# Latent attention moved beside the dense products of the last three projections, outputs as rows; the attention keeps two groups

## What is computed

```python
h = rms_norm(x, norm1[l])
proj = h @ w_in[l]
(a_cq, a_ckv, a_kr, b_q, b_k, b_v, c_q, c_k, c_v, c_qi, c_ki, c_w, d_q, d_k, d_v, d_f) = split_cols(proj)
qa = (rms_norm(a_cq, mla_q_norm[l]) @ mla_w_uq[l]).reshape(B, S, H, MLA_NOPE + MLA_ROPE)     # 64 + 32
q_a = jnp.concatenate([qa[..., :MLA_NOPE], rope(qa[..., MLA_NOPE:], pos)], axis=-1)
kv = (rms_norm(a_ckv, mla_kv_norm[l]) @ mla_w_ukv[l]).reshape(B, S, H, MLA_NOPE + MLA_V)
k_a = jnp.concatenate([kv[..., :MLA_NOPE], jnp.broadcast_to(k_rope, (B, S, H, MLA_ROPE))], axis=-1)
o_a = causal_block_attention(q_a, k_a, kv[..., MLA_NOPE:], (MLA_NOPE + MLA_ROPE) ** -0.5)   # A: latent
o_b = sliding_window_attention(q_b, k_b, v_b, swa_sinks[l], Dh ** -0.5)                      # B: window 128
o_c = dsa_attention(q_c, k_c, v_c, qi, ki, c_w, top_k, Dh ** -0.5)                           # C: 128 chosen keys
o_d = causal_block_attention(d_q, d_k, d_v, Dh ** -0.5, log_f_cum=cum)                       # D: forget gates
x = x + concat(o_a, o_b, o_c, o_d) @ w_out[l]
x = x + jnp.square(jax.nn.relu(rms_norm(x, norm2[l]) @ w_up[l])) @ w_down[l]
```

## Time and profile before

| | us |
|---|---|
| median of 3 runs | 1926.37 (1924.74 to 1927.21) |
| profiled execution | 1931.15, its span 1929.3, mean granted TensorE clock 0.979 |
| fourth, fifth, sixth job, first layer | start at 99.13, 126.56, 155.56; end at 187.93 |
| attention, first layer | 187.93 to 291.05 (103.1) |
| of it D, A, C | pair starts at about 188, 205.65; 225.57, 240.89; 254.55 |
| last scores to first product of the output job | 277.62 to 291.05 |
| attention, second layer | 873.17 to 973.64 (100.5) |

### The profile page before, as it was taken

The page is one execution under the profiler, slowest core; times in us unless marked ns, Lnnn a source line. Parts: engine busy times, 40 slices in busy tenths (PEclk is TensorE's granted clock), DMA queues, the critical chain, the costliest instruction groups (busy, mean ns, idle before and its releaser), DMA issues.

```text
span 1929.3 us, 22937 instructions
## 1 busy us (share of the span) xinstructions
PE 1852.3 (96%) x9006; PEld 1476.0 (77%) x9010; DVE 912.9 (47%) x1555; ACT 651.9 (34%) x1172; POOL 740.5 (38%) x326
## 2 busy tenths in 40 slices
PE   7999889999999999998899999999999999999997
PEld 6678557788888886786577888888788888888786
DVE  3667762424141426688624534436521124339374
ACT  4534351322121245343423222212434443443212
POOL 5232243444444443332333544444333233235342
PEclk9999899999999999997999999999999999999999
DMA  7224002232232233120024343343332222322211
GB/s 220 66 66 164 1 1 86 75 103 87 91 105 87 70 94 108 49 83 1 1 66 164 100 157 123 134 154 99 94 127 88 66 66 90 109 66 88 88 66 44
DMA packets 104441, 170.89 MB, mean 89 GB/s; under 512 B 21615, under 2 KB 39431, under 8 KB 103208
## 3 DMA queue, kind: packets, MB, share of 16 engines
q1 hardware_dynamic: 103320, 169.79, 27.0%
q10 hardware_dynamic: 1040, 0.00, 0.0%
HBM read 166.56 MB, written 7.93 MB: 90 GB/s over the span
## 4 chain that ended last, share of the span: by engine, by line
PE 88%; DVE 6%; ACT 2%; issue 2%; POOL 0%; DMA 0%; SPq 0%; DVEq 0%; ACTq 0%
PE G L2010 25%; PE G L2012 25%; PE G L2011 25%; PE S L2272 2%; PE S L1053 1%; DVE neg_max L1882 1%; DVE select L1846 1%; PE G L2308 1%; PE S L2055 1%; ACT prob L1497 1%; PE S L1027 1%; DVE work L1682 1%; PE S L1038 1%; PE G L2289 1%; DVE top L1681 1%
## 5 line engine op out<-in xcount | busy, mean ns | idle before, releaser
L1283 POOL TENSOR_TENSOR w_lo<-raw,w_hi 128x1024 fp32r<-128x1024 f32 x272 | 678.0, 2513 | 1011.2 <-ACT w_hi L1320 688.1
L1320 ACT ACTIVATE w_hi<-raw 128x2048 fp32r<-128x2048 f32 x96 | 183.8, 1915 | 543.7 <-PE G L2012 543.7
L2010 PE MATMUL G<-h_hi,w_hi 128*128 128x512 f32 x896 | 359.9, 402 | 2.1 <-DVE h_lo L810 2.1
L2012 PE MATMUL G<-h_hi,w_lo 128*128 128x512 f32 x896 | 354.8, 396 | 0.0
L2011 PE MATMUL G<-h_lo,w_hi 128*128 128x512 f32 x896 | 354.7, 396 | 0.0
L2010 PE MATMUL G<-w_hi,h_hi 128*128 128x512 f32 (+2 forms) x704 | 281.4, 400 | 6.6 <-issue 4.9
L2012 PE MATMUL G<-w_hi,h_lo 128*128 128x512 f32 (+2 forms) x704 | 272.1, 386 | 0.0
L2011 PE MATMUL G<-w_lo,h_hi 128*128 128x512 f32 (+2 forms) x704 | 271.6, 386 | 0.0
L2012 PE MATMUL G<-w_hi,u_lo 128*128 128x512 f32 x512 | 204.2, 399 | 0.0
L2010 PEld LDWEIGHTS G<-h_hi,w_hi 128*128 128x128 f32 x896 | 168.5, 188 | 45.0 <-DVE h_lo L810 2.9
L2011 PE MATMUL G<-w_lo,u_hi 128*128 128x512 f32 x512 | 201.7, 394 | 0.0
(11 more groups left out here) (314 smaller groups left out, 2247.7 us busy)
## 6 DMA issues: line engine op xcount, KB each, us to landing
raw<-in_w_in_dram SPq DMA_DIRECT2D x40, 1024.0 KB, 5.4
raw<-in_w_up_dram SPq DMA_DIRECT2D x32, 1024.0 KB, 5.3
raw<-in_w_down_dram SPq DMA_DIRECT2D x32, 1024.0 KB, 5.0
raw<-in_w_out_dram SPq DMA_DIRECT2D x12, 1024.0 KB, 5.0
w_ada<-in_w_ada_dram SPq DMA_DIRECT2D x4, 3072.0 KB, 11.9
skew_scratch<-line_scratch SPq DMA_DIRECT2D x1, 4608.0 KB
raw<-in_w_in_dram SPq DMA_DIRECT2D x8, 512.0 KB, 4.5
raw<-in_w_in_dram SPq DMA_DIRECT2D x4, 832.0 KB, 6.7
```

The lines of the kernel that those rows point to most:

```text
L1283: ins = pool.tensor_tensor(w_lo[:, c % SPLIT_SLOTS, part], raw[:, c % RAW_SLOTS, part], w_hi[:, c % SPLIT_SLOTS, part].bitcast(F32), ALU.s ...
L1320: act.activation(w_hi[:, c % SPLIT_SLOTS], raw[:, c % RAW_SLOTS], ACT.Copy).then_inc(high_ready, 1)
L2010: pe.matmul(dst, a_hi, b_hi, start=first, stop=False)
L2012: return pe.matmul(dst, a_lo, b_hi, start=False, stop=last)
```

## The change

Group A's eight items leave the attention and are hosted in the fourth to the sixth job beside B's. `SIDE` gets Q (a pair's queries or keys turned to columns, into `qkT_a`), A (an item, two steps like P) and N (its output rows `rows_oa` turned to columns). The output of A is now computed as rows, as B's is. `PAIRS` is D and C, 16 items; the last pair's query tiles run from the widest to the narrowest. M moves from the head of the attention into the jobs, and F goes last. `rows_b` is rotated in two halves, at the chores of A01 and A03 (group, pair, query tile), `rows_c` at those of P01, P02, P03, P10. 40 rounds of the index selection run ahead of the attention instead of 32. The high part of a weight piece (`MID_PIECE`) that stood at the end of the attention is made in two parts at items 2 and 4 and its low part in four behind POOL's scalings 5, 6, 7 and 9.

```diff
-PAIRS = [(g, hp) for g in "DAC" for hp in range(2)]
-ITEMS = [(p, qt) for p in range(len(PAIRS)) for qt in range(TT)]
+PAIRS = [(g, hp) for g in "DC" for hp in range(2)]
+ITEMS = [(p, TT - 1 - n if p == len(PAIRS) - 1 else n) for p in range(len(PAIRS)) for n in range(TT)]
...
-EARLY_SPLITS = {20: (0,), 21: (1,), 22: (2,), 23: (3,)}
+MID_HIGH = {2: slice(0, 2), 4: slice(2, 4)}
+MID_LOW = {5: 0, 6: 1, 7: 2, 9: 3}
+MID_PIECE = 2 * (JOB_V + 1) + 1
+EARLY_SPLITS = {NI - 4: (0,), NI - 3: (1,), NI - 2: (2,), NI - 1: (3,)}
...
-SIDE = ([("L",)] + [("U", t) for t in range(TT)] + [("K",)]
-        + [("P", hp, qt) for hp in range(2) for qt in range(TT)] + [("F",), ("M",)])
+SIDE = ([("L",)] + [("U", t) for t in range(TT)]
+        + [item for hp in range(2) for item in
+           [("Q", hp, "q"), ("Q", hp, "k")] + [("A", hp, qt) for qt in range(TT)]]
+        + [("K",)] + [("P", hp, qt) for hp in range(2) for qt in range(TT)] + [("N",), ("M",), ("F",)])
 NS = len(SIDE)
 AT = {item: n for n, item in enumerate(SIDE)}
-NB = 2 * TT
+NB = 4 * TT
...
-          JOB_B: {1: 1, 6: 1, 11: 1, **spread(12, 32, side_steps(0, AT["K",]))},
-          JOB_C: spread(14, 32, side_steps(AT["K",], AT["K",] + 3)),
-          JOB_D: spread(0, 32, side_steps(AT["K",] + 3, AT["K",] + 6)),
-          JOB_V: spread(0, 32, side_steps(AT["K",] + 6, AT["M",]))}
+          JOB_B: {1: 1, 6: 1, 11: 1, **spread(12, 32, side_steps(0, AT["Q", 0, "q"]))},
+          JOB_C: spread(1, 32, side_steps(AT["Q", 0, "q"], AT["A", 1, 0])),
+          JOB_D: spread(0, 32, side_steps(AT["A", 1, 0], AT["P", 0, 2])),
+          JOB_V: spread(0, 32, side_steps(AT["P", 0, 2], NS + 1))}
 LAYER_SC = NB + NI
 LAYER_OV = NI
-EARLY_ROUNDS = 2 * ROUNDS
+EARLY_ROUNDS = 5 * ROUNDS // 2
...
+            def part_low(number, c, k):
+                pool.wait_ge(high_ready, number + 1)
+                ins = pool.tensor_tensor(w_lo[:, c % SPLIT_SLOTS, k], raw[:, c % RAW_SLOTS, k],
+                                         w_hi[:, c % SPLIT_SLOTS, k].bitcast(F32), ALU.subtract)
+                if k == HALF_K - 1:
+                    ins.then_inc(low_ready, 1)
...
+                    if i in MID_LOW:
+                        part_low(number + MID_PIECE, MID_PIECE, MID_LOW[i])
+                for c in range(MID_PIECE + 1, FIRST_GROUP_PIECE):
...
+                    elif kind == "Q":
+                        scale = LATENT_SCALE if SIDE[n][2] == "q" else 1.0
+                        ins = act.activation(latent_columns(n, 1), bank(n, 1)[0:MLA_QK], ACT.Copy, scale=scale)
                     else:
-                        ins = act.activation(mixT_bc[:, 1, :], bank(n, 1), ACT.Copy)
+                        dst = mixed("B" if kind == "M" else "A", 1)
...
+                def part_high(part):
+                    c = MID_PIECE
+                    act.wait_ge(raw_loaded[c % RAW_SLOTS], l * LAYER_LOADS[c % RAW_SLOTS] + loads_upto(c))
+                    act.wait_ge(bank_filled, (jobs + PROJ_JOBS) * TT)
+                    ins = act.activation(w_hi[:, c % SPLIT_SLOTS, part], raw[:, c % RAW_SLOTS, part], ACT.Copy)
+                    if part.stop == HALF_K:
+                        ins.then_inc(high_ready, 1)
...
-                    if i == NI - 1:
-                        ahead(JOB_V, 1)
+                    if i in MID_HIGH:
+                        part_high(MID_HIGH[i])
...
-                    if n == AT["K",] - 1:
-                        stored(JOB_B)
-                        rotate(rows_b[:, :, 0:384].rearrange("p t (h d) -> p t h d", h=6), rope64, 6, 32)
-                        dve.engine_nop().then_inc(window_ready, 1)
-                    if n == AT["K",] + 3 and not output:
+                        if t == TT - 1:
+                            dve.engine_nop().then_inc(latent_ready, 1)
+                    if n in (AT["A", 0, 1], AT["A", 0, 3]) and not output:
+                        first = 2 if n == AT["A", 0, 3] else 0
+                        if not first:
+                            stored(JOB_B)
+                        rotate(rows_b[:, :, 0:384].rearrange("p t (h d) -> p t h d", h=6), rope64, 6, 32, first, first + 2)
+                        if first:
+                            dve.engine_nop().then_inc(window_ready, 1)
+                    if n == AT["P", 0, 1] and not output:
                         stored(JOB_C)
-                    if output and AT["K",] + 3 <= n <= AT["K",] + 2 + TT:
-                        rotate_c(n - AT["K",] - 3)
+                    if output and n - AT["P", 0, 1] in range(TT):
+                        rotate_c(n - AT["P", 0, 1])
...
+                        dst = rows_oa[:, qt, P * hp:P * hp + P].rearrange("p (h d) -> p h d", h=2)
...
+                def side_scores(n):
+                    kind, hp, qt = SIDE[n]
+                    tiles = side_tiles(n)
+                    q, k = slice(P * qt, P * qt + P), slice(P * tiles[0], P * (qt + 1))
+                    if kind == "P" and n == AT["K",] + 1:
                         pe.wait_ge(even_taken, evens + (EVEN[n - 1, "t"] + 1))
+                    elif kind == "A" and qt == 0:
+                        pe.wait_ge(even_taken, evens + (EVEN[n - 1, "s"] + 1))
+                    if qt == 0 and not scored(n - 1):
                         pe.wait_ge(odd_taken, odds + (ODD[n - 1, "s"] + 1))
                     for e in range(2):
-                        at = slice(HD * e, HD * e + HD)
-                        pe.matmul(bank(n, e)[:, 0:P * len(tiles)], qkT_b[at, 2 * hp, P * qt:P * qt + P],
-                                  qkT_b[at, 1, P * tiles[0]:P * (qt + 1)], start=True, stop=False)
-                    mask = window_few[:, 0 if qt else P:2 * P]
+                        if kind == "A":
+                            queries, keys = (qkT_a[hp][e + at][0:MLA_QK] for at in (0, 2))
+                        else:
+                            queries, keys = (qkT_b[HD * e:HD * e + HD, at, :] for at in (2 * hp, 1))
+                        pe.matmul(bank(n, e)[:, 0:P * len(tiles)], queries[:, q], keys[:, k], start=True, stop=False)
...
+                    kind, hp, _ = SIDE[n]
+                    tiles = side_tiles(n)
                     for e in range(2):
+                        rows, at = (mla_v, HD * (2 * hp + e)) if kind == "A" else (rows_b, 384 + HD * e)
                         for b, kb in enumerate(tiles):
                             ins = pe.matmul(bank(n, 0)[:, HD * e:HD * e + HD], prob_b[n % 2][e][:, P * b:P * b + P],
-                                            rows_b[:, kb, 384 + HD * e:384 + HD * e + HD], start=b == 0, stop=b == len(tiles) - 1)
+                                            rows[:, kb, at:at + HD], start=b == 0, stop=b == len(tiles) - 1)
...
-                assert AT["M",] % 2 and AT["M",] == NS - 1
                 give_qk(0, range(qk_units(0)))
-                advance(1)
-                pe.wait_ge(odd_taken, odds + (ODD[AT["M",], "s"]))
+                pe.wait_ge(odd_taken, odds + ODDS)
                 give_scores(0)
-                pe.wait_ge(even_taken, evens + EVENS)
-                pe.wait_ge(odd_taken, odds + ODDS)
```

165 lines of the change are left out of this document (92 added, 73 removed).

## The result

The changed kernel took 1932.57 us (median of 9 runs, 1928.89 to 1934.09) against 1926.50 (9 runs): a ratio of 1.0027, 95% interval 1.0018 to 1.0036, so about 5 us slower by the ratio, 6 by the medians. The profiled execution took 1930.56 us, span 1928.7, mean clock 0.979, which is no slower than the profiled execution before (1931.15).

What follows compares the result with a forecast made beforehand. PE's stream was taken as the bound (88% of the chain), plus its few waits. Terms of -4.5 us in the first layer and -2.4 in the second gave -6.9, from the median 1926.37 to 1919.5; range 1909 to 1932.

Steps and rivals of the forecast that it cites:

- D's second pair: Attention: fewer transposes to host and no index rounds after the fourth item; -5.2 us first layer, -1.6 second.
- GpSimd's low parts: Attention: four low parts of the weight piece between GpSimd's scalings, one delaying the next item; +0.3 us a layer.
- Group A: -29.0: Attention: the section of group A's eight items disappears, -29.0 us a layer.
- +27.3 of PE work: Fourth to sixth job: group A's items, Q, N and M return between dense products, +27.3 us a layer.
- The waits on DVE: Hosting jobs: PE waits for DVE slowed by rotations, +4.2 us in the sixth, +1.8 in the fourth, a layer.
- The 1.0 for meetings of a rotation with a weight split: Sixth job: rotations slowed from 0.42 to 2.60 us beside GpSimd's weight split; 1.0 us allowed of 2.2.
- F at the end, +0.6, less 0.4: Head of the attention: F last leaves DVE and ACT less time, M gone saves 0.4; net +0.2 us.
- From one execution to the median: Whole kernel: 1924.2 us from the profiled execution, less 4.8 for the median of runs, gives 1919.5.
- The tail, -4.1: Last scores to output job: 13.4 becomes 7.6 us, against scores coming 1.7 later; net -4.1 us.
- The signs: Disproof: job waits above 9.5 us a layer, clock below 0.95 in fourth or fifth job, tail over 11 us.
- DVE as the bound at 13.5 us of waits: Rival, the jobs: items outpace DVE, PE waits 13.5 us a layer instead of 6; 1934.5 us, chance 0.14.
- The second rival: No net gain: half the gain of tail and D's second pair stays a DVE wait; 1927 us, chance 0.25.

Runs made afterwards that it cites:

- e1: The kernel before, unchanged, run and profiled a second time: median 1927.52 us, this profiled execution 1926.84 us.
- e13: The changed kernel, unchanged, run and profiled a second time: median 1930.74 us, ratio 1.0017 to before.
- e8: The changed kernel with 45 of the 48 index rounds a layer left out, so group C attends to wrong keys: 1899.49 us.
- e12: e2 with all 48 index rounds ahead of the attention instead of 32: 1925.11 us.
- e7: The changed kernel with its hosted steps dealt 13, 13, 14 to the last three jobs instead of 12, 12, 16: 1923.67 us, ratio 0.9989 to before.
- e6: The kernel before with only the weight piece's high and low parts made inside the attention: 1918.39 us, ratio 0.9952.
- e3: The changed kernel with the reversed last pair and the weight piece's split inside the attention both undone: 1942.10 us, ratio 1.0071 to before.
- e2: The kernel before with only the reversed last pair and the weight piece split inside the attention: 1915.19 us, ratio 0.9938.

## Why the prediction was wrong

It said 1919.5, range 1909 to 1932, faster at 0.52; measured 1932.57. The step that failed most is D's second pair, -5.2 and -1.6 us: it started from a stretch that was slow by the clock (19.92 us, 17.54 in e1), left out that DVE has more to do in D's first two items than in A's (2.7 us) and took the end of the half clock as given (4.6 us in one layer of two). The second is the head of the attention with F uncovered, +0.2, which measured +1.7 to +3.1. The ledger against e1, the execution of before that lies near the median:

| us | forecast | first layer | second layer |
|---|---|---|---|
| fourth job to the first scores | +33.5, +32.0 | +36.8 (128.70 - 91.87) | +38.2 (130.10) |
| GpSimd's low parts | +0.3 | in the rows below | in the rows below |
| D, first pair | 0 | 0.0 | +0.1 |
| D, second pair | -5.2, -1.6 | +3.4 (20.94 - 17.54) | -1.2 |
| group A | -29.0 | -29.0 | -29.0 |
| C, first pair | 0 | -1.7 (12.78 - 14.49) | -1.7 |
| C, second pair and tail | -4.1 | -5.5 (16.69 - 22.17) | -5.7 |
| sum | -4.5, -2.4 | +4.1 | +0.9 |

+4.9 in all. The two executions compared differ by 3.6 us in their spans (1928.7, 1925.1), so -1.3 lie outside these stretches, in pieces of up to 2 us of either sign; the ratio of all runs, 1.0027, is +5.2.

- **"Group A: -29.0" and "+27.3 of PE work"** held. Summed over PE's timeline, the hosted blocks without their waits grew by 27.6 us in the first layer (18.0 to 45.6), and by 26.8 in the first layer of e13, where no block lies at the half clock. Queries, scores and outputs came near their forecast prices: 0.79 for eight transposes, 4.3 against 4.5 for a pair's scores, 4.1 for a pair's outputs.
- **The waits on DVE, "6.0"**, measured 5.1 and 4.1 more than before, and 6.5 in the first layer of e13, where the clock is full: PE's slow stretches and its waits take each other's place, since DVE sets the sixth job's length (43.4 of 45.35 us busy). In the fourth A01's rotation cost 0.8 and A03's nothing, where I had 1.0 and 0.8. The 1.0 for meetings of a rotation with a weight split was wrong in place: none of the 36 instructions of the rotations took over 0.56 us. The split met the two-column addition instead, and PE's wait behind it is 1.7.
- **Missing from the sum: the interval behind a block.** I priced a block up to the next dense start, but the interval behind that is 0.32 and not 0.23; the earlier trace rows end at that start. 39 blocks instead of 17: +2.0 us a layer.
- **"F at the end, +0.6, less 0.4"**: wrong in size. From the start of the last dense product to the first scores, before takes 4.17 us, the changed kernel 5.9 in the first layer and 7.3 in the second, where the clock is 0.76 under F. That is +1.7 and +3.1 where I had +0.2. In the first layer PE waits there 0.57 us for DVE's `fox_k` and 0.89 for its `qkT`, where e1 has 0.32 for `qkT` alone. The dip of the clock in the sixth job, which looks like a second missing term, costs nothing: the job is as long without it.
- **"D's second pair, -5.2"**: the step that failed most. First, 19.92 was no fair measure of before: e1 has 17.54. Second, A's second pair was no fair measure of what would be left. Its last two items take the same 5.59 us as those of D's second pair in the quick form, but its first two 8.07 where D's take 10.75 at either clock: DVE is busy for 7.78 us there with three index rounds in it, and for 10.00 with four in D's. With no rounds D's two items take 7.67 (e8) and 8.17 (e12, first layer). What I added to A's 13.7, 1.0 and 2.2 us, I had put down to the clock; it is 2.7, and it is DVE's. Third, I took the end of the half clock as given, and the last two items lie at the full clock or the half, 5.59 or 10.19 us. So the pair is 13.7 + 2.7 = 16.3, or 4.6 more. Quick form against quick form, the lighter pair is worth 1.2 us (17.54 to 16.34), near my -1.6 for the second layer; slow against slow it is 1.0 longer. What picks the one or the other was not settled: e7's profile has neither layer slow, which is too few to say that dealing the steps differently avoids it.
- **From one execution to the median.** I subtracted the 4.8 us by which the profiled execution exceeded the median, and counted as gains two stretches in which that execution was slow (2.4 of D's pair, 1.5 of the second layer's sixth job). These 3.9 us were in effect counted twice.
- **"The tail, -4.1"** was right in mechanism and somewhat too small. Against e1 the stretch from the last scores to the output job fell from 13.59 to 7.20 us, -6.4 where I had -5.8, and these scores came 0.9 later, not 1.7: -5.5. e6 shows that the weight piece is the larger part. The 1.7 us of C's first pair, forecast at nothing, e3 gives without the tail edits.
- **The signs.** Those that would make the prediction wrong did not come: PE's waits were 6.1 and 5.2 us a layer, the clock 1.00 in the fourth and fifth job, the last scores to the output job 7.2. The expected sizes held for the jobs (123.05 against 122) and not for the attention, 70.7 and 67.3 us from the last dense product on against 65 and 66. The list had no sign for the head or for D's pairs, where it failed.
- **The rivals.** DVE as the bound at 13.5 us of waits is not what happened, though in the sixth job alone DVE is the bound. The second rival, in which half of the gain in tail and D's second pair stays a wait on DVE, is right for D's pair, whose first two items DVE sets; the tail gave all. A rival in which the half clock gets worse in the attention, not in the jobs, was missing.

The version that beats both is e2: before with the two tail edits, 12 us under before and 17 under the changed kernel. Against e7, the quickest form of the move that keeps the whole computation, it is 8 us ahead.

## What to carry to other kernels

Work of PE that is moved between dense products keeps its price: what can be won is only the idle time of the section it leaves (here 3.4 of 29 us), and 22 more interruptions at 0.09 us, five us of waiting and a slower head ate more than that. A half-clock stretch has a price only where PE is the limit: look at the busy times before putting it into a sum. Where a change bundles several edits, price each against the profile as if alone; here two of them were worth 12 us and were hidden by the third. And before a stretch is used as a measure, look at the same stretch in the other layer: 19.9 beside 17.5 for the same instructions is a sign of the clock, not of work.
